# Adding weighted expert rows to the residual in DRAM by scatter, in place of storing them and gathering at the end

## The reference

```python
h = rmsnorm(x, norm_ffn);  x = x + hier_moe(h, ...)
return rmsnorm(x, norm_final)

def hier_moe(h, w_group, w_router, w_exp_gate, w_exp_up, w_exp_down):
    gl = (t @ w_group); gp = softmax(gl); gi = argmax(gl)           # one of 4 groups
    gw = gp[gi]; esel = (t @ w_router)[group gi]                    # 4 experts in it
    tv, ti = lax.top_k(esel, 2);  tw = softmax(tv) * gw             # two experts per token
    for e in range(16):
        he = silu(t @ w_exp_gate[e]) * (t @ w_exp_up[e])            # 1024 -> 256
        out = out + dense_w[:, e:e + 1] * (he @ w_exp_down[e])      # 256 -> 1024, weighted
```

## Time and profile before

| what | value |
|---|---|
| median of 3 runs | 938.31 us |
| the profiled execution, its own time | 938.0 us |
| its span, first to last instruction | 936.2 us |
| mean granted TensorE clock | 0.958 |
| busy: TensorE, DVE, ACT, POOL | 836.3, 468.7, 391.8, 189.7 us |
| moved by DMA | 142.44 MB, mean 152 GB/s |
| last matmul begins | 892.91 us |

### The profile page before, as it was taken

The page is one execution under the profiler, slowest core; times in us unless marked ns, Lnnn a source line. Parts: engine busy times, 40 slices in busy tenths (PEclk is TensorE's granted clock), DMA queues, the critical chain, the costliest instruction groups (busy, mean ns, idle before and its releaser), DMA issues.

```text
span 936.2 us, 13270 instructions
## 1 busy us (share of the span) xinstructions
PE 836.3 (89%) x5002; PEld 710.9 (76%) x5002; DVE 468.7 (50%) x778; ACT 391.8 (42%) x540; POOL 189.7 (20%) x131
## 2 busy tenths in 40 slices
PE   3999999999999999999999999999849899999910
PEld 3988878898788888878888888888737687778700
DVE  4511355454419632324231247533586888877537
ACT  4522244344432543333334113134425677668413
POOL 0001010000000001100100001300013487777543
PEclk9999999999999999999999999999859899999965
DMA  9215131322121313221220212893858899998675
GB/s 292 77 46 127 47 74 46 74 65 53 31 75 37 91 46 71 77 68 46 29 80 13 89 46 94 249 363 112 315 186 312 315 370 378 389 303 287 227 274 211
DMA packets 97261, 142.44 MB, mean 152 GB/s; under 512 B 4507, under 2 KB 75371, under 8 KB 97163
## 3 DMA queue, kind: packets, MB, share of 16 engines
q1 hardware_dynamic: 89276, 115.04, 36.6%
q0 software_dynamic: 7904, 26.44, 10.2%
q10 hardware_dynamic: 32, 0.26, 0.2%
HBM read 116.31 MB, written 25.43 MB: 151 GB/s over the span
## 4 chain that ended last, share of the span: by engine, by line
PE 74%; DVE 8%; DMA 6%; ACT 5%; issue 4%; SPq 2%; POOL 2%; ACTq 0%; POOLq 0%; DVEq 0%
PE main L828 20%; PE main L830 19%; PE main L829 19%; PE work L865 2%; PE work L895 2%; PE work L928 2%; PE work L912 2%; DMA expert_rows<-y_sb 1%; PE work L1076 1%; ACT prob_t L1200 1%; PE work L882 1%; DVE x L1867 1%; PE work L1031 1%; DMA raw<-in_w_in 1%; DMA e_raw<-in_w_exp_down 1%
## 5 line engine op out<-in xcount | busy, mean ns | idle before, releaser
L1440 DVE TENSOR_TENSOR w_lo<-raw,w_hi 128x2048 fp32r<-128x2048 f32 x30 | 68.7, 2290 | 259.8 <-ACT w_hi L1144 259.8
L828 PE MATMUL main<-ht_hi,w_hi 128*128 128x512 f32 (+1 forms) x576 | 196.9, 342 | 0.0
L829 PE MATMUL main<-ht_lo,w_hi 128*128 128x512 f32 (+1 forms) x576 | 193.9, 337 | 0.0
L830 PE MATMUL main<-ht_hi,w_lo 128*128 128x512 f32 (+1 forms) x576 | 193.8, 336 | 0.0
L828 PEld LDWEIGHTS main<-ht_hi,w_hi 128*128 128x128 f32 x576 | 109.2, 190 | 18.7 <-issue 4.7
L829 PEld LDWEIGHTS main<-ht_lo,w_hi 128*128 128x128 f32 x576 | 109.3, 190 | 11.6
L830 PEld LDWEIGHTS main<-ht_hi,w_lo 128*128 128x128 f32 x576 | 109.2, 190 | 11.7
L828 PE MATMUL main<-w_hi,ht_hi 128*128 128x256 f32 (+1 forms) x304 | 95.9, 315 | 3.4 <-DVE ht_lo L1457 3.4
L678 POOL DMA_DIRECT2D bias<-bias_vectors x16 | 12.4, 773 | 426.8 <-DVE nmx L1500 183.6
L830 PE MATMUL main<-w_hi,ht_lo 128*128 128x256 f32 (+1 forms) x304 | 93.5, 308 | 0.0
L829 PE MATMUL main<-w_lo,ht_hi 128*128 128x256 f32 (+1 forms) x304 | 93.5, 307 | 0.0
(11 more groups left out here) (262 smaller groups left out, 1518.9 us busy)
## 6 DMA issues: line engine op xcount, KB each, us to landing
e_raw<-in_w_exp_gate SPq DMA_DIRECT2D x16, 1024.0 KB, 8.2
e_raw<-in_w_exp_up SPq DMA_DIRECT2D x16, 1024.0 KB, 9.1
e_raw<-in_w_exp_down SPq DMA_DIRECT2D x16, 1024.0 KB, 8.5
raw<-in_w_in SPq DMA_DIRECT2D x28, 512.0 KB, 4.6
expert_rows<-y_sb SPq DMA_DIRECT2D x19, 512.0 KB, 8.0
raw<-in_w_in SPq DMA_DIRECT2D x9, 1024.0 KB, 5.2
expert_rows<-y_sb SPq DMA_DIRECT2D x1, 5632.0 KB, 22.4
raw<-in_w_out SPq DMA_DIRECT2D x4, 1024.0 KB, 6.0
```

The lines of the kernel that those rows point to most:

```text
L828: pe.matmul(out, s_hi, m_hi, start=(first and i == 0), stop=False)
L829: pe.matmul(out, s_hi, m_lo, start=False, stop=False)
L830: last = pe.matmul(out, s_lo, m_hi, start=False, stop=(final and i == n - 1))
L1440: dve.tensor_tensor(w_lo[:, c % 2, :], raw[:, c % 2, :], w_hi[:, c % 2, :], ALU.subtract).then_inc(s_wlo, 1)
```

## The change

The expert rows are no longer stored. Each expert tile's 128 rows, already weighted, are added to their tokens' rows of `x1_dram` by one indirect DMA with an adding write (`add_rows`), issued by POOL between the gather of phase j and the split of phase j, for tile j-2. Since a token stands in two expert tiles, each add waits until the add before it has landed. Unused slots go to 128 spare rows behind the tokens. At the end SP waits for the last two adds and reloads x1, and the final norm runs on it; the twelve gathers, the sums and the fill with zeros are gone.

The weight is put into the hidden rows: the factor 0.5 of L1805 becomes a column `weights` per tile, made by a second set of twelve matmuls (`weight_table`) between the gate/up product and the hidden transposes of tile 0. So the weights must be known by tile 0: `weight_differences` moves ahead of the table's evacuation, the two Exp ahead of the first rows, `route_weights` into DVE's tile 0. The 24 one-hot instructions become six with broadcast operands; token numbers are stored plus one so that an empty slot is known by 0.

```diff
+            def add_rows(r, j):
+                if j >= 3 or not isinstance(r, int):
+                    ids = back_column[:, j % 2:j % 2 + 1]
+                    gp.tensor_copy(ids, back_u[:, bass.ds(r * 2 + j, 1)]).then_inc(s_backcol, 1)
+                    gp.wait_ge(s_backcol, r * 2 + j)
+                    gp.sem_inc(s_adds, 1)
+                else:
+                    ids = back_u[:, j:j + 1]
+                gp.wait_ge(s_y, r * 2 + (j + 1))
+                gp.sem_inc(s_adds, 1)
+                if late(r, j, 1):
+                    gp.wait_ge(s_added[(j - 1) % 2], r * 16 + 16 * ((j - 1) // 2 + 1))
+                    gp.sem_inc(s_adds, 1)
+                gp.indirect_dma_start(x1_dram.ap(), bass.IndirectOffsetOnAxis(ap=ids, axis=0), y_sb[:, j % 2, :], None,
+                                      compute_op=ALU.add).then_inc(s_added[j % 2], 16)
...
             with gp.Fori(0, loops) as r:
                 for j in (3, 4):
                     gather(r, j + 2)
+                    add_rows(r, j - 2)
                     split_lo_part(r, j, 2)
+            add_rows(loops, 1)
             split_lo_part(loops, 3, 2)
+            add_rows(loops, 2)
             split_lo_part(loops, 4, 2)
-            gp.wait_ge(s_ystored, 2)
-            for t in range(NT):
-                for k in range(2):
-                    gp.indirect_dma_start(yg[:, t, k, :], None, y_dram.ap(), ...
+            add_rows(loops, 3)
+            add_rows(loops, 4)
...
             def tile(r, j):
                 load_tile(r, j + 4, (0, 1))
-                store_y(r, j - 1)
                 load_tile(r, j + 3, (2,))
...
+            sp.wait_ge(s_added[0], loops * 16 + 16 * 3)
+            sp.sem_inc(s_adds, 1)
+            sp.wait_ge(s_added[1], loops * 16 + 16 * 2)
+            sp.sem_inc(s_adds, 1)
             for t in range(NT):
+                sp.dma_start(x1[:, t, :], x1_dram.ap()[P * t:P * t + P, :]).then_inc(s_x1back[t], 16)
...
+            def weight_table():
+                pe.wait_ge(s_hotw, 2)
+                for i in range(2 * NT):
+                    k, t = divmod(i, NT)
+                    last = pe.matmul(main[1][:, 512 + TILES_PAD:512 + 2 * TILES_PAD], hot_slot[:, k, t, :].bitcast(F32),
+                                     hot_weight[:, k, t, :], start=(i == 0), stop=(i == 2 * NT - 1))
+                last.then_inc(s_wtable, 1)
...
                 gate_up(r, j)
+                if not late(r, j, 1):
+                    weight_table()
...
+                for k in range(2):
+                    rt(dve.tensor_tensor(hot_weight[:, k, :, :], ... ALU.is_equal))
+                    dve.tensor_tensor(hot_weight[:, k, :, :], hot_weight[:, k, :, :],
+                                      over(wt[:, k, :], [P, NT, TILES_PAD], 2), ALU.mult).then_inc(s_hotw, 1)
+                dve.wait_ge(s_wtable, 1)
+                rt(dve.tensor_scalar(weights[:, :], main[1][:, 512 + TILES_PAD:512 + 2 * TILES_PAD], 0.5, None, ALU.mult))
...
+                dve.tensor_copy(weight_column[:, par:par + 1], weights[:, column_j]).then_inc(s_wcol, 1)
                 dve.wait_ge(s_tanh, r * 2 + (j + 1))
...
-                dve.scalar_tensor_tensor(he[:, par, :], he[:, par, :], 0.5, ps[:, DE:2 * DE], ALU.mult, ALU.mult).then_inc(s_he, 1)
+                dve.scalar_tensor_tensor(he[:, par, :], he[:, par, :], weight_column[:, par:par + 1], ps[:, DE:2 * DE],
+                                         ALU.mult, ALU.mult).then_inc(s_he, 1)
...
                 if late(r, j, 2):
-                    dve.wait_ge(s_yout[j % 2], r * 16 + 16 * (j // 2))
+                    dve.wait_ge(s_added[j % 2], r * 16 + 16 * (j // 2))
                 dve.tensor_copy(y_sb[:, j % 2, :], main[1][:, :]).then_inc(s_y, 1)
...
             def tile(r, j):
                 rows_lo(r, j + 1)
+                if not late(r, j, 1):
+                    route_weights()
                 hidden(r, j)
```

More of the change, by code:

```diff
@@ L754, in _ @@
             loops = loop_count(gp)
-            for j in (3, 4):
-                gather(0, j)
+            gather(0, 3)
+            gather(0, 4)
+            gp.wait_ge(s_back, 1)
+            add_rows(0, 0)
             split_lo_part(0, 2, 2)
@@ L1739, in _, with weight_differences @@
             rt(dve.tensor_copy(slots_f[:, :, :, :], slots_u[:, 1:3, :, :]))
-            for k in range(2):
-                for t in range(NT):
-                    dve.tensor_scalar(hot_tile[:, k, t, :], small[:, C_IOTA:C_IOTA + TILES_PAD], slots_f[:, 1, k, t:t + 1],
-                                      small[:, C_TOKEN + t:C_TOKEN + t + 1], ALU.is_equal, ALU.mult)
-                    dve.tensor_scalar(hot_slot[:, k, t, :], small[:, C_IOTA:C_IOTA + P], slots_f[:, 0, k, t:t + 1],
-                                      None, ALU.is_equal).then_inc(s_hot_slot, 1)
+            def weight_differences():
+                rt(dve.tensor_reduce(value(0), gl, AX.X, ALU.max))
+                dve.tensor_tensor(four(3), gl, over(value(0), [P, NT, 4], 2), ALU.subtract).then_inc(s_diffs, 1)
+                rt(dve.tensor_reduce(value(2), four(5), AX.X, ALU.max))
+                rt(dve.scalar_tensor_tensor(four(7), best, LOWEST, four(5), ALU.mult, ALU.add))
+                rt(dve.tensor_reduce(value(6), four(7), AX.X, ALU.max))
+                dve.tensor_tensor(value(4), value(6), value(2), ALU.subtract).then_inc(s_diffs, 1)
@@ new lines, in _ @@
+            for k in range(2):
+                rt_on(dve.tensor_tensor(hot_tile[:, k, :, :], over(slots_f[:, 1, k, :], [P, NT, TILES_PAD], 2),
+                                        over(small[:, C_IOTA:C_IOTA + TILES_PAD], [P, NT, TILES_PAD], 1), ALU.is_equal))
+                rt_on(dve.tensor_tensor(hot_slot[:, k, :, :], over(slots_f[:, 0, k, :], [P, NT, P], 2),
+                                        over(small[:, C_IOTA:C_IOTA + P], [P, NT, P], 1), ALU.is_equal))
+                dve.wait_ge(s_rt, count[0])
+                dve.tensor_tensor(hot_tile[:, k, :, :], hot_tile[:, k, :, :],
+                                  over(small[:, C_TOKEN:C_TOKEN + NT], [P, NT, TILES_PAD], 2), ALU.mult).then_inc(s_hot_slot, 1)
@@ L1796, in hidden @@
             def hidden(r, j):
+                par = j % 2
+                column_j = bass.ds(r * 2 + j, 1) if late(r, j, 3) else slice(j, j + 1)
+                dve.tensor_copy(weight_column[:, par:par + 1], weights[:, column_j]).then_inc(s_wcol, 1)
                 dve.wait_ge(s_tanh, r * 2 + (j + 1))
@@ L1859, in _ @@
             dve.wait_ge(s_gain3, 16)
-            dve.wait_ge(s_x1back, 16 * NT)
             for t in range(NT):
-                dve.wait_ge(s_yg[t], 32)
-                for k in range(2):
-                    if k == 0 and t >= SHARED:
-                        dve.wait_ge(s_added, t - SHARED + 1)
-                        continue
-                    dve.scalar_tensor_tensor(x1[:, t, :], yg[:, t, k, :], wt[:, k, t:t + 1], x1[:, t, :],
-                                             ALU.mult, ALU.add).then_inc(s_comb, 1)
-                    dve.wait_ge(s_comb, combined(t) - (1 - k))
-                if t >= 1:
-                    finish(t - 1)
-            finish(NT - 1)
+                finish(t)
     return nc
```

114 lines of the change are left out of this document (41 added, 73 removed).

## The result

The changed kernel takes 964.88 us (median of 4 runs, 964.53 to 967.24) where the kernel before takes 938.78 beside it: ratio 1.0284, 95% interval 1.0265 to 1.0303. The span grew from 936.2 to 962.7. It is slower, as forecast, and inside the stated range of 929 to 968, but by 26.1 us, not by 11.7.

The account below looks back on a forecast made before the run. POOL, nearly as full as TensorE in the expert loop, would collide with DVE and set the round. Loop +27.6, routing -3.5 and tail -11.4 gave +12.7 on a 936.2 us span, rounded to 950 us; range 929 to 968.

Parts of the forecast that it names:

- The round on POOL: Expert loop: an added column, wait and issue make POOL and DVE collide every round, 12.3 us in place of 9.3.
- The sum of 12.3: Loop round: DVE's pair 4.49, gather issue rest 0.9, add's column 0.97, its issue 1.0, handovers 0.3, POOL's split 4.6.
- the loop term: Expert loop: +18.6 us over eight tiles and +9 over the rounds after, in all +27.6.
- The start: Routing and first tiles: early weights save up to 6.4 us, the weight table costs 1.8; kept -3.5, bounds -4.6 and 0.
- gives a part back: First tiles: POOL's second split waits for the first add, 2.8 us later than it began, returning part of the saving.
- The transfers: DMA: an add lands in about 8 us, range 4.6 to 15.2; the half megabyte replaces the store, so no cost.
- a landing below the round costs nothing: Loop DMA: the add before must land before the next issue, so landings under the 12.3 us round are free.
- The tail: Behind the last matmul: two adds, reload and six norms sum to 31.5 us against 42.9, -11.4; bounds -14 and -4.
- The faster one: Rival in the loop: POOL and DVE rounds never collide, 10.2 us a round, 931 us in all; chance 0.28.
- Adds that pace the loop: Rival in the loop: adds need over 12.3 us to land; at 13.5, 966 us; chance 0.1.
- The clock: Rival in the loop: TensorE's idle time lowers its clock, adding 1 us on 13 rounds, 963 us; chance 0.07.

Follow-up runs that it names:

- the plain scatter: Changed kernel with the scatter writing the rows instead of adding them (sum with x1 left out): 952.66 us, ratio 1.0158.
- the version with both edits: Changed kernel with each add issued behind its split and both index columns made by VectorE instead of GpSimd: 941.9 us, ratio 1.0041.

## Why the prediction was right in direction and short by half

**The round on POOL** was the right mechanism: its columns last 2.8 us, DVE's pair is stretched, rounds of 12.8. The sum of 12.3 had the add's issue at 1.0 us, by the undisturbed gather; an accumulating issue takes 1.6, and the plain scatter's 1.0 in the same place shows where the 0.6 comes from. POOL's thirteen rounds from 746.80 on were put at 154.2 us (ten at 12.3, three at 10.4) and take 160.3: most of the 7.2 us by which the loop term was short (27.6 forecast, 34.8 measured). The steady round was otherwise put together as it runs. What the step did not see is that the order makes a ring of the same length beside it: I named the split queued behind the add as the cause of the collision, and took the sum along POOL. Moving the columns away, or the split forward, each gave next to nothing; both together gave 23 us.

**The start** failed: -3.5 forecast, +3.4 measured. The early weights were sized well (up to 6.4; 6.4 measured). The weight table was put at 1.8 us from eight matmuls of 0.97; it is 24 instructions and 2.87 us, with its wait and the clock of the tile behind it 5.1 at tile 4. The main miss is the sentence that POOL's second split, waiting for the first add, "gives a part back": 1.1 us were kept for it. The adds cost 6.2 there: tile 4 begins at 736.59 with the early weights and broadcast rows and no adds, and at 742.81 in the changed kernel without its table. The split is not only late (729.49 instead of 722.08 with the table); behind it the column and the gather's issue collide with DVE as they do in the loop, and TensorE waits for the rows. Of the routing, the broadcast rows, put at nothing, gave 1.5. So 744.5 - 6.4 - 1.5 + 6.2 + 5.1 is the measured 747.9, where the forecast had -6.4 + 1.8 + 1.1. Taken in another order the shares shift: with the add behind that split and the columns off POOL, table in place, tile 4 begins at 740.11, 7.8 earlier.

The start is 6.9 us off and the loop 7.2; these two, less 0.3 in the tail, are the 13.8 us by which the span's forecast was short.

**The transfers.** That a landing below the round costs nothing was right, as the chain of adds in the loop shows. That the adding itself costs the loop nothing held only because POOL was slower still: beneath the 20 us that the two edits took out of the loop lie 11 that the accumulating transfers take (163.7 against 152.7). The Trainium skill (Collectives: The Full Stack, The bandwidth ceiling) has a reducing transfer between cores read two sources and run at half a copy's rate; the traces here agree, with 1.5 us of the engines more per add, about what its bytes take once more, 354 against 380 GB/s at the same share, and landings of 6.0 against 3.3 us at the least.

**The tail** came out right, -11.7 against -11.4, in part by luck: its adds land in 6 us, not 5, and the first norm starts 14.8 us behind the last matmul's end, not 13.4; the norms repeat every 1.82 us, not 2.15, which gives that back.

**The rivals.** The faster one fell: rounds never came free of collisions. Adds that pace the loop: not in this kernel, but in the version with both edits they pace the tail. The clock: behind TensorE's pauses it did fall in the loop, to a mean of 0.92 (0.77 in tile 4, behind the pause of 4.02 us), and the matmuls' 15 us more come with it. But the eight rounds on POOL keep to 12.77 us through stretches at 0.77 and at 1.00, with no idle time to wait in, so the matmuls' length does not set them. That the 966 and 963 of these two rivals lie nearer to the measured 964.9 than the forecast's 950 is chance.

## What to carry to other kernels

When an engine is full, look for a second chain of the same length before you expect a gain from shortening the first: here one edit alone was worth under 2 us, the other under 2, the two together 23. Ask of each wait put in front of other work what that work holds up, and whether this comes round to the wait again. A faster end is paid for wherever its work is moved to, and the price there is set by what that stage has left: POOL, busy only 20% of the whole span, had 1.65 us to spare in a loop tile of 9.30, and was given over 2 us more.

## What the runs showed of the hardware that was not expected

An indirect DMA issue on POOL is held up by DVE's splits as a copy is: with no column copies left on POOL, the gather's issue behind the split took 2.85 us against 0.98 undisturbed, while DVE's pair ran. The Trainium skill (SBUF — State Buffer, SBUF: two separate sides) tells of an exclusive lock between the two engines for a DVE instruction with two inputs in SBUF against a POOL instruction that reads it; the runs agree for instructions and for this issue. An accumulating scatter of 128 rows of 4 KB takes 1.6 us to issue and at the least 6.0 to land; the same scatter without adding, 1.0 and 3.3. An instruction of POOL may be shown as starting some 0.55 us before the issue ahead of it is through, and its own time is then longer by that: the split at 793.30 starts before the add's issue ends at 793.86, and lasts 5.19 us where it lasts 4.63 behind a plain issue.
